# Forgetting attention: the product with the values once per head, with the values as the stationary operand

## The reference, cut to what matters

```python
def forgetting_attention(q, k, v, logf, valid):
    B, H, P, hd = q.shape
    nb = P // BLOCK                       # BLOCK = 128, H = 16, hd = 64
    c = jnp.cumsum(logf, axis=-1)
    kpos = jnp.arange(P)
    scale = hd ** -0.5

    def block(i):
        s0 = i * BLOCK
        qb = lax.dynamic_slice_in_dim(q, s0, BLOCK, axis=2)
        cb = lax.dynamic_slice_in_dim(c, s0, BLOCK, axis=2)
        logits = jnp.einsum('bhqd,bhkd->bhqk', qb, k) * scale + cb[..., None] - c[:, :, None, :]
        qpos = s0 + jnp.arange(BLOCK)
        allowed = (kpos[None, :] <= qpos[:, None]) & (valid[None, :] | (kpos[None, :] == qpos[:, None]))
        p = jax.nn.softmax(jnp.where(allowed[None, None], logits, NEG), axis=-1)
        return jnp.einsum('bhqk,bhkd->bhqd', p, v)
...
    y_a = forgetting_attention(q_a, k_a, v_a, logf, valid)
    y_a = y_a.transpose(0, 2, 1, 3).reshape(B, P, FOX_W).astype(dt)
...
    mixed = g_a * (y_a @ w_o_fox) + g_b * (y_b @ w_o_ret)
```

## Time and profile before

| | us |
|---|---|
| three runs: lowest, median, highest | 3606.66, 3607.4, 3607.8 |
| profiled execution: time, span | 3611.76, 3610.0 |
| TensorE busy in the span (matmul) | 3343.3 |
| granted TensorE clock, mean over the span (share of full speed) | 0.966 |
| the attention's 64 units | from 751 to 996 |

### The profile page before, as it was taken

One profiled execution on the slowest core, in us unless ns is written; L12 is line 12 of the kernel. 1 busy time (PEld: TensorE's weight loads), 2 busy tenths in 40 slices (PEclk: granted clock), 3 DMA queues, 4 the chain that ended last, 5 costly groups with the idle time before them and its releaser, 6 DMA issues. The chain is left out here.

```text
span 3610.0 us, 60740 instructions
## 1 busy us (share of the span) xinstructions
PE 3343.3 (93%) x25218; PEld 3106.9 (86%) x25234; DVE 1626.6 (45%) x2684; ACT 1330.7 (37%) x2349; POOL 489.6 (14%) x466
## 2 busy tenths in 40 slices
PE   6999999999999899998999859999995999869997
PEld 6999997877788899987988849999994799769996
DVE  3666533444434456664356452222224447433233
ACT  3222322255533322234257453121215448442222
POOL 1010010144400010010014001000000114010000
PEclk9999999999999999998999979999997999879998
DMA  3444321110022344541100102121210211113221
GB/s 135 166 171 173 123 81 61 63 49 30 19 84 92 97 140 169 181 145 52 59 24 31 39 17 63 59 64 60 63 59 20 75 48 31 48 53 94 88 92 49
DMA packets 82126, 285.82 MB, mean 79 GB/s; under 512 B 8832, under 2 KB 13184, under 8 KB 81728
## 3 DMA queue, kind: packets, MB, share of 16 engines
q1 hardware_dynamic: 77584, 266.96, 22.6%
q0 software_dynamic: 3840, 14.47, 1.2%
q10 hardware_dynamic: 432, 0.52, 0.0%
HBM read 279.82 MB, written 2.10 MB: 78 GB/s over the span
## 5 line engine op out<-in xcount | busy, mean ns | idle before, releaser
L1950 DVE TENSOR_TENSOR r_Wbasel<-r_Wf,r_Wbaseh 128x1024 fp32r<-128x1024 f32 (+1 forms) x269 | 338.8, 1261 | 636.3 <-ACT r_Wbaseh L1406 636.0
L1406 ACT ACTIVATE r_Wbaseh<-r_Wf 128x1024 fp32r<-128x1024 f32 (+1 forms) x269 | 279.6, 1041 | 559.9 <-PE PS L924 469.1
L922 PE MATMUL PS<-r_X1h,r_Wbaseh 128*128 128x264 f32 (+2 forms) x1216 | 391.8, 322 | 17.0 <-DVE r_Wbasel L1950 11.3
L923 PE MATMUL PS<-r_X1l,r_Wbaseh 128*128 128x264 f32 (+2 forms) x1216 | 379.4, 312 | 0.0
L924 PE MATMUL PS<-r_X1h,r_Wbasel 128*128 128x264 f32 (+2 forms) x1216 | 378.7, 311 | 0.0
L922 PE MATMUL PS<-r_X2h,r_Wbaseh 128*128 128x256 f32 (+1 forms) x1200 | 365.2, 304 | 9.5 <-DVE r_X2l L2094 5.5
L924 PE MATMUL PS<-r_X2h,r_Wbasel 128*128 128x256 f32 (+1 forms) x1200 | 357.2, 298 | 0.0
L923 PE MATMUL PS<-r_X2l,r_Wbaseh 128*128 128x256 f32 (+1 forms) x1200 | 355.8, 296 | 0.0
L1950 DVE TENSOR_TENSOR r_Wtopl<-r_Wf,r_Wtoph 128x1024 fp32r<-128x1024 f32 (+1 forms) x140 | 171.1, 1222 | 222.2 <-ACT r_Wtoph L1406 222.0
L922 PEld LDWEIGHTS PS<-r_X1h,r_Wbaseh 128*128 128x128 f32 x1216 | 231.6, 190 | 41.2 <-DVE r_Wbasel L1950 15.0
L922 PE MATMUL PS<-r_X2h,r_Wtoph 128*128 128x256 f32 x880 | 251.0, 285 | 9.1 <-DVE r_Wtopl L1950 9.1
(11 more groups left out here) (361 smaller groups left out, 9205.0 us busy)
## 6 DMA issues: line engine op xcount, KB each, us to landing
r_Wf<-in_wmod SPq DMA_DIRECT2D x96, 512.0 KB, 3.6
r_Wf<-in_f_in SPq DMA_DIRECT2D x88, 512.0 KB, 4.4
r_Wf<-in_g_in SPq DMA_DIRECT2D x88, 512.0 KB, 3.5
r_Wf<-in_f_out SPq DMA_DIRECT2D x32, 448.0 KB, 4.2
r_Wf<-in_g_out SPq DMA_DIRECT2D x32, 448.0 KB, 3.2
r_Wf<-in_f_out SPq DMA_DIRECT2D x16, 512.0 KB, 4.4
r_Wf<-in_w_o SPq DMA_DIRECT2D x16, 512.0 KB, 3.5
r_Wf<-in_g_out SPq DMA_DIRECT2D x16, 512.0 KB, 3.5
```

Of the source, the lines that this page charges most:

```text
L922: self.e.matmul(o, wh, xh, start=first, stop=False)
L923: self.e.matmul(o, wh, xl, start=False, stop=False)
L1406: e.activation(p.w(i, cols)[0], p.Wf[:, i % NW, 0:cols], ACT.Copy).then_inc(*p.hi.did(i))
L1950: e.tensor_tensor(l, p.Wf[:, i % NW, 0:cols], h.bitcast(F32), ALU.subtract).then_inc(*p.lo.did(i))
```

## The change

1. The rows of exponentials are multiplied by the reciprocal of their sum in place, on VectorE, before they are turned (`scale_rows`); reciprocal and scaling of unit u - 1 are done in turn u. The turning waits for this scaling and no longer for the exponential alone. Pb holds four units, one of each size.
2. The 16 meta columns are turned by a transpose and not by a matmul with the identity.
3. ScalarE copies a unit's turned blocks to a place of its own in PT, and the turned meta columns to MT, so that the four units of a head lie side by side. From head 1 on it waits for the product of the head before.
4. The product is done once per head (`head_values`), in the turn after the last unit of the head was turned, and ahead of that turn's turning. The 64 columns of the head's values are the stationary operand; the turned exponentials stream with up to 256 columns. Query blocks 0 and 3 go to the tile of columns 0 to 63, blocks 1 and 2 to the tile of columns 64 to 127, by turns.
5. Two copies on VectorE per head write the result as features to YA (`head_outputs`). The YTF buffer, the 32 transposes, the eight copies and the barrier "foxed" go. YA lies where YTF lay.
6. `FOX_PLAN` has other unit numbers, and its offset is 14 in place of 12.

```diff
+FOX_PLACE = [0, 3, 1, 2]
+FOX_TURNED = [0, 5, 7, 1]
-FOX_PLAN = [(0, "project", "q", 0, 0, 3), (1, "project", "q", 0, 3, 6), (2, "project", "q", 0, 6, 8),
-            (3, "root", "q", 0), (3, "project", "k", 0, 0, 4), (4, "refine", "q", 0),
-            (4, "project", "k", 0, 4, 8), (5, "root", "k", 0), (5, "project", "k", 1, 0, 4),
-            (6, "scale", "q", 0), (6, "refine", "k", 0), (6, "project", "k", 1, 4, 8), (7, "root", "k", 1),
-            (8, "scale", "k", 0), (8, "refine", "k", 1), (10, "scale", "k", 1), (10, "stack", 0), (14, "stack", 1)]
+FOX_PLAN = [(0, "project", "q", 0, 0, 3), (1, "project", "q", 0, 3, 6), (2, "project", "q", 0, 6, 8), (3,
+            "project", "k", 0, 0, 4), (4, "root", "q", 0), (4, "project", "k", 0, 4, 8), (5, "refine", "q", 0),
+            (6, "root", "k", 0), (6, "project", "k", 1, 0, 4), (7, "project", "k", 1, 4, 8), (7, "scale", "q",
+            0), (7, "refine", "k", 0), (9, "root", "k", 1), (9, "scale", "k", 0), (10, "refine", "k", 1), (12,
+            "scale", "k", 1), (12, "stack", 0), (15, "stack", 1)]
-    steps = sorted(((8 * m - 12 + u, m, *f) for m in range(8) for u, *f in FOX_PLAN), key=lambda x: x[0])
+    steps = sorted(((8 * m - 14 + u, m, *f) for m in range(8) for u, *f in FOX_PLAN), key=lambda x: x[0])
...
+    def products(self, h):
+        p, v = self.p, h * 64
+        PT = p.PT
+        for j in range(5):
+            w = p.VF[:, j + 1, v:v + 64] if j < 4 else p.VF[0:NMETA, 0, v:v + 64]
+            if j == 4:
+                yield 0, w, p.MT[:, 0:256], 0, 256
+                yield 64, w, p.MT[:, 256:512], 0, 256
+                continue
+            if j == 0:
+                yield 0, w, PT[:, 0:256], 0, 256
+            else:
+                a = 128 * (FOX_TURNED[3] + j)
+                yield 0, w, PT[:, a:a + 128], 128, 256
+            a = 128 * (FOX_TURNED[1] + j)
+            if j < 2:
+                yield 64, w, PT[:, a:a + 512].rearrange("p (s x) -> p s x", x=256)[:, :, 0:128], 0, 256
+            elif j == 2:
+                a = 128 * (FOX_TURNED[2] + j)
+                yield 64, w, PT[:, a:a + 128], 128, 256
...
 # TensorE
+            if A.joined and u > A.lag and A.units[u - A.lag - 1].head_done:
+                self.head_values(A, u - A.lag - 1)
+            if A.lag <= u < n + A.lag:
+                self.turned(A, u - A.lag)
...
-        e.wait_ge(*p.act.of(("exp", A.id, u)))
+        e.wait_ge(*(p.dve.of(("scaled", A.id, u)) if A.joined else p.act.of(("exp", A.id, u))))
...
-                t = e.matmul(p.psb2(b, 512, 640, w), A.Pb[:, u % 3, c:c + w], p.IDF, start=True, stop=True)
+                t = e.transpose(p.psb2(b, 512, 640, w), A.exps(u, c, c + w), p.IDF)
...
+    def head_values(self, A, u):
+        p, e = self.p, self.e
+        h = A.units[u].h
+        b = self.take(("c", A.id, h), (p.dve, ("o", A.id, h)), part="c")
+        e.wait_ge(*p.act.of(("pt", A.id, u)))
+        steps = list(A.products(h))
+        for n, (r, w, x, a, z) in enumerate(steps):
+            t = e.matmul(p.PS[r:r + 64, b, a:z], w, x, start=n < 2, stop=n >= len(steps) - 2)
+        t.then_inc(*p.mm.did(("c", A.id, h)))
...
 # ScalarE
+        if A.joined:
+            if d.h >= 1:
+                e.wait_ge(*p.mm.of(("c", A.id, d.h - 1)))
+            whole, rest = A.turned(d)
+            e.activation(whole, p.psb2(b, 0, n), ACT.Copy).then_inc(*p.act.did())
+            e.activation(rest, p.psb2(b, 512, 640, NMETA), ACT.Copy).then_inc(*p.act.did(("pt", A.id, u)))
+            return
...
 # VectorE
+            if A.joined:
+                if 1 <= u <= n:
+                    self.sums(A, u - 1)
+                    self.scale_rows(A, u - 1)
+                if u > A.lag and A.units[u - A.lag - 1].head_done:
+                    self.head_outputs(A, u - A.lag - 1)
+                continue
...
+    def scale_rows(self, A, u):
+        p, e = self.p, self.e
+        x = A.exps(u, 0, A.units[u].n)
+        e.wait_ge(*p.dve.of(("rc", A.id, u)))
+        e.tensor_scalar(x, x, p.SM[:, 8 + 2 * (u % 4):9 + 2 * (u % 4)], None, ALU.mult).then_inc(
+            *p.dve.did(("scaled", A.id, u)))
+
+    def head_outputs(self, A, u):
+        p, e = self.p, self.e
+        h = A.units[u].h
+        b, r = p.bank(("c", A.id, h)), 64 * (h % 2)
+        y = p.YA[r:r + 64, h // 2, :].rearrange("p (i n) -> p i n", n=128)
+        e.wait_ge(*p.mm.of(("c", A.id, h)))
+        e.tensor_copy(y[:, 0:4:3, :], p.PS[0:64, b, 0:256].rearrange("p (i n) -> p i n", n=128)).then_inc(
+            *p.dve.did())
+        e.tensor_copy(y[:, 1:3, :], p.PS[64:128, b, 0:256].rearrange("p (i n) -> p i n", n=128)).then_inc(
+            *p.dve.did(("o", A.id, h)))
...
-        self.bar("foxed")
-        self.features(p.YTF, range(4), range(8), ("ya",), lambda f: (p.act, ("ya", f)),
-                      lambda f: [(p.dve, ("o", "fox", 63))])
         self.bar("ya")
...
-        self.bar("foxed")
-        self.fence("foxed")
-        for f in range(8):
-            e.wait_ge(*p.mm.of(("ya", f)))
-            e.activation(p.YA[:, f, :], p.psb(p.bank(("ya", f))), ACT.Copy).then_inc(*p.act.did(("ya", f)))
         self.bar("ya")
```

More of the change, by code:

```diff
@@ L745, in __init__ @@
         self.n, self.h, self.i, self.half, self.blocks, self.ready = n, h, i, half, blocks, ready
-        self.out, self.add, self.bias, self.hooks = out, add, bias, []
+        self.out, self.add, self.bias, self.hooks, self.head_done = out, add, bias, [], False
 class FoxUnits:
     def __init__(self, p):
-        self.p, self.id, self.l, self.Pb, self.PT, self.units = p, "fox", None, p.Pb, p.PT, []
+        self.p, self.id, self.l, self.units, self.joined, self.lag, self.slots = p, "fox", None, [], True, 2, 4
         late = fox_steps(False)
@@ L766, in __init__ @@
                          + [(0, NMETA, p.VF[0:NMETA, 0, v:v + 128])],
-                         stacked_fox(p, h) + [(p.dve, "cumulated")], p.YTF[:, i, h * 64:h * 64 + 64], add)
+                         stacked_fox(p, h) + [(p.dve, "cumulated")], None, add)
+                d.head_done = i == 3
                 d.hooks = [("fox", *x[1:]) for x in late if x[0] == 4 * h + i]
@@ L773, in qk, with exps, turned @@
         return p.QS[:, s, c:c + 128], p.KS[:, s, a:z], p.KL[:, s, a:z]
+    def exps(self, u, a, z):
+        o = [0, 144, 416, 816][u % 4]
+        return self.p.Pb[:, o + a:o + z]
+    def turned(self, d):
+        a = 128 * FOX_TURNED[d.i]
+        m = 128 * FOX_PLACE.index(d.i)
+        return self.p.PT[:, a:a + 128 * (d.i + 1)], self.p.MT[:, m:m + 128]
+    def products(self, h):
[18 more added lines that the diff above has]
+                yield 64, w, PT[:, a:a + 128], 128, 256
 class LatentUnits:
     def __init__(self, p, l):
-        self.p, self.id, self.l, self.Pb, self.PT, self.units = p, f"l{l}", l, p.PbA, p.PTA, []
+        self.p, self.id, self.l, self.PT, self.units, self.joined, self.lag = p, f"l{l}", l, p.PTA, [], False, 2
+        self.slots = 3
         self.last, self.out_by = {}, {}
@@ L830, in qk, with exps @@
         return p.QSA[:, s, c:c + 128], p.KSA[:, ks, k0 + a:k0 + z], p.KLA[:, ks, k0 + a:k0 + z]
+    def exps(self, u, a, z):
+        return self.p.PbA[:, u % 3, a:z]
 class Engine:
@@ L1250, in attention @@
     def attention(self, A):
-        for u in range(len(A.units) + 3):
-            if u < len(A.units):
+        n = len(A.units)
+        for u in range(n + A.lag + 1):
+            if u < n:
                 self.scores(A, u)
[L1254 to L1257, removed]
+            if A.joined and u > A.lag and A.units[u - A.lag - 1].head_done:
+                self.head_values(A, u - A.lag - 1)
+            if A.lag <= u < n + A.lag:
+                self.turned(A, u - A.lag)
+            if not A.joined and u > A.lag:
+                self.values(A, u - A.lag - 1)
     def scores(self, A, u):
@@ L1283, in turned @@
             if w == 128:
-                t = e.transpose(p.psb2(b, j * 128, j * 128 + 128), A.Pb[:, u % 3, c:c + 128], p.IDF)
+                t = e.transpose(p.psb2(b, j * 128, j * 128 + 128), A.exps(u, c, c + 128), p.IDF)
                 j += 1
             else:
-                t = e.matmul(p.psb2(b, 512, 640, w), A.Pb[:, u % 3, c:c + w], p.IDF, start=True, stop=True)
+                t = e.transpose(p.psb2(b, 512, 640, w), A.exps(u, c, c + w), p.IDF)
         t.then_inc(*p.mm.did(("b", A.id, u)))
@@ L1714, in attention @@
         self.log_tables()
-        for u in range(len(A.units) + 3):
-            if u < len(A.units):
+        n = len(A.units)
+        for u in range(n + A.lag):
+            if u < n:
                 for hook in A.units[u].hooks:
                     self.hook(A, *hook)
-            if 2 <= u <= len(A.units) + 1:
-                self.turned(A, u - 2)
-            if u < len(A.units):
+            if u >= A.lag:
+                self.turned(A, u - A.lag)
+            if u < n:
                 self.exp(A, u)
@@ L2327, in attention @@
     def attention(self, A):
```

(15 more changed lines are left out.)

18 lines of the change are left out of this document (8 added, 10 removed).

## The result

The changed kernel takes 3567.7 us (median of four, 3562.64 to 3568.31), the kernel before 3607.19. The ratio is 0.9887, 95% interval 0.9870 to 0.9905: by the ratio 41 us less. The profiled execution took 3568.31 us (span 3566.5), 43.5 less than the profiled one of before. Forecast were 52 less.

What follows compares the result with a forecast made beforehand. TensorE was taken to bound the kernel. 3.46 us less per head, 55.4 over 16 heads, with +3 and +4 for waits, -1 start and -3 end, gave -52.4 us: 3555 us, range 3543 to 3568 (chance 0.72).

Steps and rivals of the forecast that it cites:

- signs of being wrong: Product over 3 us, TensorE waiting on scaling beyond the last heads or over 5 us on POOL's stack, clock under 1.00.
- signs of being right: Product in 2.0 to 2.3 us, turning in 1.5 to 2.3, last scores some 50 us earlier, full clock in the stage.
- Values, once per head: TensorE's products with the values, done once per head: 2.1 us against 4.66, 2.56 us less per head.
- rival of tiles in turn: The two 64-column tiles run one after the other, losing 1.5 us per head, 24 us: 3579 us; chance 0.10.
- Turning: TensorE's turning of the exponentials: 1.9 us per head, 0.9 less; lower end 1.50, upper end 2.3.
- The 6.8 us that I gave away: In the turning: if 16-column transposes were still two records, 64 x 0.107 = 6.8 us of gain would stay away.
- VectorE "priced at nothing": Added VectorE work, 16 us, priced at nothing, except late scalings in the last heads (3 us) and hook waits (4 us).
- rival in which the other engines become the bound: ScalarE, VectorE and POOL bound the attention; 0.35 us more wait per unit brings 22 us back: 3577 us; chance 0.11.
- The clock: Rival: the attention's clock falls, 6.8 us more per head at the lower level, up to 3664 us; chance 0.05.
- The start: Ahead of the attention, half a k projection fills the sum of squares' wait for ScalarE: 1 us gained.
- The end: From last scores to the mix: 6.2 us in place of 11.5; net of what the per-head sum counted, 3 us gained.

Runs made afterwards that it cites:

- tiles_in_turn: Changed kernel with a head's nine products reordered: the five of one 64-column tile first, then the four of the other; ratio 0.9922 to the kernel before.
- spread: Changed kernel with the root of q in step 5, its refinement in step 6 and its scaling in step 8; 3558.7 us, ratio 0.9857.
- pool_narrow: Changed kernel with most of POOL's refinements and stacks cut to 32 columns, leaving out needed work, so no candidate; ratio 0.9849.
- fill_tail: Changed kernel with 28 unread matmuls of 512 columns (6.4 us) added from unit 52 on, where TensorE waits; ratio 0.9863.
- meta_alone: Kernel before with one edit: the 16 meta columns turned by a transpose, not a matmul with the identity; 3586.81 against 3610.37 us, ratio 0.9932.
- spread_fill: Changed kernel with root, refinement and scaling of q in steps 5, 6 and 8, plus unread matmuls in the last 12 units; 3554.07 us, ratio 0.9847.
- refine_late: Changed kernel with POOL's refinement of q in step 6 of the plan and not 5; ratio 0.9874 to the kernel before.

## Why the prediction was right or wrong

The direction, the range and TensorE as the bound of the kernel before were right. The 52 us were 41, as a difference of larger errors that offset each other: 14 us more gained in products and turning, 13 more lost in waits and up to 10 in the clock. That the time came out inside the forecast's own range, at its upper edge, is in part luck. (The ends that the prediction names for that range add up to 3542 and 3575, not to 3543 and 3568.) Two of its signs of being wrong came true: waits for the scaling in more than the last heads, and a clock under 1.00. Of its signs of being right, the last scores came 38 us earlier and not some 50, and product and turning were shorter than its bounds of 2.0 and 1.5 us.

- **Values, once per head.** Right in kind, 1.81 us against 2.1, which is 4.6 us more gained. The rival of tiles in turn is refuted by tiles_in_turn.
- **Turning.** Mis-sized: 1.30 us per head and not 1.9, below my lower end of 1.50, since a transpose of 16 columns holds up what follows by 0.02 to 0.11 us. That is 9.6 us more gained. The Trainium skill (TensorEngine Tiling (Array Packing), Feature Incompatibilities) says that column tiling excludes the fp32 transpose. The 6.8 us that I gave away at the upper end by it did not show up: the transpose of 16 columns stands as one record, as for full width.
- **VectorE "priced at nothing".** The step that failed. I looked for late scalings only in the last heads. They are late once per pair in the middle too, at unit 8m - 3, because its scaling stands behind the stack, root and maximum, and then behind POOL; and I took the duration of the scaling from a row in which POOL was idle. 3 + 4 us forecast, 20 measured. spread and pool_narrow show both halves. The rival in which the other engines become the bound had this loss at nearly its size (22 us), but as a little in each of the 64 units; measured were 22 waits, the long ones once per pair and at both ends of the stage.
- **The clock.** A rival at 0.05 that came true in part: 20 us at the lower level, up to 10 us lost. The last product shows the price: 3.38 us at the lower level, 1.81 at the full one (fill_tail, spread). My argument against it, that a wait of 1.4 us had not lowered it, was one case; there are ten waits of 1.3 us or more now, and the clock fell near some of them (755, 855, 910, 925 us) and stayed full at others (802 and 829). What decides is open. The Trainium skill (TensorE: Matmul & The Clock Gate, Part 4: PE-mode transpose) says that transposes don't count as busy the way matmuls do. No run here separates transposes from waits, but meta_alone and spread_fill have all 224 transposes of the stage and a full clock.
- **The start.** 1 us gained was forecast. The new list puts POOL's refinement of q ahead of the barrier, and ScalarE waits 4.0 us there for it and VectorE 5.5. TensorE pays 3.5 of it by the first head's product (refine_late). I counted TensorE's moved steps and not POOL's.
- **The end.** 958.51 - 950.50 = 8.0 us from the last scores to the mix, 6.2 forecast; the lower clock is 1.6 of it.

## What to carry to other kernels

Split a change into its parts and price each where the engine is the bound: here one line was worth 24 us and the large rewrite 16 on top of it, because the rewrite left TensorE with less work than the engines that feed it need for theirs. Once the bound engine has slack, the order within the other engines' lists decides, and a move that gives one wait more room (a lag of three, the scaling first) can make another longer. A matmul engine that begins to wait can lose its clock as well, and it fell at other places even where two kernels run the same list, so a few us between two profiled executions prove little. Unread matmuls in waits that were there anyway cost nothing; whether they gained anything is open.

## What the runs showed of the hardware

- VectorE's multiplication of fp32 rows in SBUF by a scalar per row does not run beside POOL's operations on SBUF: for 272 columns it took 1.23 us when it began together with one of 1.04, and ended 0.15 us behind it; alone it took 0.36.
- Matmuls for two 64-column tiles of the array overlapped when they stood in the list by turns, and not when each tile's stood in a row: 1.81 against 3.60 us for the same nine products.
- The identity matmul of 16 columns cost 0.37 us per unit more than a transpose of them, by 24 us over 64 units. By starts it is 0.31 in the turning and 0.10 in the product behind.
- The lower clock made the last product take 3.38 us in place of 1.81.
